# A one-core diffusion trunk on Trainium2: one weight load waits for a scatter, four matmul units change their place

## The reference

```python
for i in range(DEPTH):                                   # 4
    sh1, sc1, g1, sh2, sc2, g2 = split(silu(c) @ w_mod[i] + b_mod[i], 6)
    x = x + g1 * mixer_i(rmsnorm(x, norm_mix[i]) * (1 + sc1) + sh1)
    h = rmsnorm(x, norm_ffn[i]) * (1 + sc2) + sh2
    s = sigmoid(h @ w_router)                            # 384 x 16
    # best group of 4 experts, then the best two inside it; weights s, normalised
    # expert e: (silu(h @ w_gate[e]) * (h @ w_up[e])) @ w_down[e], 1024 -> 256 -> 1024
    x = x + g2 * sum_over_the_two_experts(weight * expert(h))
```

## Time and profile before

| | us |
|---|---|
| median of 3 runs | 1728.62 |
| lowest, highest | 1721.64, 1734.59 |
| the profiled execution | 1723.16 |
| its span, first to last instruction | 1721.3 |
| PE busy in the span | 1462.2 (85%) |
| mean granted clock of TensorE | 0.939 of full |

### The profile page before, as it was taken

One profiled execution on the slowest core, in us unless ns is written; L12 is line 12 of the kernel. 1 busy time (PEld: TensorE's weight loads), 2 busy tenths in 40 slices (PEclk: granted clock), 3 DMA queues, 4 the chain that ended last, 5 costly groups with the idle time before them and its releaser, 6 DMA issues.

```text
span 1721.3 us, 26508 instructions
## 1 busy us (share of the span) xinstructions
PE 1462.2 (85%) x10765; PEld 880.4 (51%) x10765; DVE 543.2 (32%) x1326; ACT 374.3 (22%) x985; POOL 197.5 (11%) x287
## 2 busy tenths in 40 slices
PE   2889897898997998598889988978989899979983
PEld 1766685232576676233374455843326666763321
DVE  0125624111526525011333343231105145251104
ACT  0104512111212622111120343211112035221101
POOL 0100021000213012010110000210101000120002
PEclk9899998899998998899999999978999999979987
DMA  9797045999959124799948323458998850358992
GB/s 343 268 321 262 2 150 195 362 420 422 323 218 318 22 98 157 314 399 420 393 172 274 70 74 127 143 234 306 422 418 297 268 191 2 123 203 302 421 413 100
DMA packets 125060, 428.70 MB, mean 249 GB/s; under 512 B 13124, under 2 KB 55063, under 8 KB 100359
## 3 DMA queue, kind: packets, MB, share of 16 engines
q1 hardware_dynamic: 96854, 350.32, 53.2%
q0 software_dynamic: 21136, 72.73, 12.6%
q10 hardware_dynamic: 6944, 3.91, 0.8%
HBM read 389.22 MB, written 40.26 MB: 250 GB/s over the span
## 4 chain that ended last, share of the span: by engine, by line
PE 66%; DMA 14%; DVE 8%; issue 5%; ACT 2%; POOL 2%; SPq 1%; DVEq 0%; ACTq 0%; POOLq 0%
PE bank L1666 58%; DMA work<-in_moe_w_gate 4%; DMA ring<-in_w_mod 4%; DMA h_slots<-xn,row_of 3%; PE bank L1829 3%; PE bank L1988 2%; DMA hT<-h_slots 1%; PE bank L1723 1%; ACT pp L1018 1%; POOL small L692 1%; POOL h_slots L797 1%; DVE xn L1165 1%; PE bank L1874 1%; DVE hT L1152 1%; SPq L602 1%
## 5 line engine op out<-in xcount | busy, mean ns | idle before, releaser
L1666 PE MATMUL bank<-ring,pp 128*32 128x512 f32 x2312 | 321.2, 604 | 11.3 <-issue 9.2
L1666 PE MATMUL bank<-ring,hT 128*128 128x256 f32 (+3 forms) x1142 | 271.3, 397 | 5.9 <-DVE hT L1152 3.3
L1666 PEld LDWEIGHTS bank<-ring,hT 128*128 128x128 f32 x1142 | 212.9, 195 | 61.2 <-issue 29.0
L1666 PE MATMUL bank<-work,pp 128*32 128x512 f32 x888 | 239.7, 624 | 2.7 <-DVE pp L1540 2.0
L1666 PE MATMUL bank<-ring,xn 128*128 128x256 f32 x768 | 168.2, 380 | 0.0
L1666 PEld LDWEIGHTS bank<-ring,pp 128*32 128x32 f32 x2312 | 88.5, 111 | 135.3 <-issue 134.3
L1666 PEld LDWEIGHTS bank<-ring,xn 128*128 128x128 f32 x768 | 145.0, 190 | 19.4
L1666 PE MATMUL bank<-V,pp 128*32 128x512 f32 x640 | 121.8, 623 | 25.5 <-issue 21.5
L1556 DVE TENSOR_TENSOR pp<-bank,pp 128x256 f32<-128x256 f32 x40 | 17.0, 425 | 339.2 <-ACT pp L1095 339.2
L1666 PE MATMUL bank<-ring,condT 128*32 128x256 f32 x1536 | 98.7, 403 | 17.2 <-DMA ring<-in_w_mod 17.2
L1018 ACT ACTIVATE pp<-bank,neg_max 128x384 f32<-128x384 f32 x192 | 95.6, 514 | 13.9 <-DVE neg_max L1447 10.1
(11 more groups left out here) (249 smaller groups left out, 1562.0 us busy)
## 6 DMA issues: line engine op xcount, KB each, us to landing
ring<-in_w_mod SPq DMA_DIRECT2D x96, 1024.0 KB, 8.9
ring<-in_moe_w_down SPq DMA_DIRECT2D x52, 1024.0 KB, 18.7
ring<-in_moe_w_gate SPq DMA_DIRECT2D x32, 1024.0 KB, 13.0
ring<-in_moe_w_up SPq DMA_DIRECT2D x32, 1024.0 KB, 15.3
hT<-h_slots POOLq DMA_DIRECT2D x36, 512.0 KB, 11.3
V<-in_moe_w_gate SPq DMA_DIRECT2D x16, 1024.0 KB, 13.7
V<-in_moe_w_up SPq DMA_DIRECT2D x16, 1024.0 KB, 17.0
work<-in_moe_w_gate SPq DMA_DIRECT2D x16, 1024.0 KB, 9.8
```

Source lines behind the costliest of these rows:

```text
L1666: return pe.matmul(out, lhsT, rhs, start=start, stop=stop)
```

## The change

SP waits for `h_out` of the layer (all six scatters landed) ahead of the gate unit of expert 3, in all four layers. On PE the first four "route" units run behind `hrow(2)` and ahead of the count of loads; the second four stay behind the ranks.

```diff
@@ sync
                 for key in moe_units(L):
+                    if key == ("moe_g", L, 3):
+                        sp.wait_ge(h_out, 96 * (L + 1))
                     if key[0] == "mod":
                         fill_mod(key)
                         continue
@@ tensor
                 hrow(2)
+                mods(mod_of["route"][:4])
                 pe.wait_ge(gates_ready, L + 1)
                 key = ("load", L)
...
                 done(mm(job_bank(key)[:, 32:48], ones[:, :], g48[:, 0:16], False, True))
-                mods(mod_of["route"])
+                mods(mod_of["route"][4:])
                 pe.wait_ge(mod_copied, min(6 * L + 8, 24))
```

## The result

| | us |
|---|---|
| after, median of 12 runs (lowest, highest) | 1715.1 (1706.2, 1720.4) |
| before beside it, median of 12 runs | 1728.7 |
| ratio, 95% interval | 0.9911 (0.9895 to 0.9927) |
| the profiled execution after | 1713.5, span 1711.7, clock 0.945 |

The change gains 0.89% (0.73 to 1.05), 15.4 us (12.6 to 18.2), against the 19.7 forecast. That ratio is one of means; the two medians lie 13.5 us apart. The direction and the mechanism held, the size came out a fifth smaller (by the medians a third), and the gain stays just short of 1%.

What follows compares the result with a forecast made beforehand. PE waits for block 1's gather behind a scatter slowed by SP's weights. 11.9 + 9.8 + 0.6 - 1.6 - 1.0 = 19.7 us takes the profiled 1723.2 to 1703.5, the median 1728.6 to 1709; range 1695 to 1727 (8 in 10).

Steps and rivals of the forecast that it cites:

- scatter in, layer 0: Last scatter of layer 0 lands at 301.7 instead of 302.3, gain 0.6 us; the hold has no grip there.
- layer 1: Last scatter of layer 1 lands at 694.6 instead of 706.5, with fewer weights beside it: gain 11.9 us.
- layer 2: Last scatter of layer 2 lands at 1150.8 instead of 1160.65, with fewer weights beside it: gain 9.8 us.
- gathers of layers 0 to 2: Block 1's gather stays at 8 us, again meeting a full SP queue (bounds 4.5 and 9): no gain.
- block 1 in layer 3: Three held loads run beside layer 3's gather, so block 1's gate-up starts later: loss 1.6 us (bounds 0 and 4).
- clock: After PE's idle time, block 1's gate-up in layers 1 and 2 runs slower, about 0.5 us each: loss 1.0.
- Rival (a): PE stays at half clock through the four early units, count 3.5 us late: gain 12.2, 1716.4 us; chance 0.17.
- Rival (c): Block 1's gather lands behind all 3.1 MB of released weights: 33 us lost against 21 gained, 1740 us; chance 0.08.
- Rival (b): Four weight units ahead still slow the scatter to its end: gain 2.9 us in all, 1726 us; chance 0.2.
- part 1: Four units moved ahead of the count on PE: count 1 us later (bounds 0 and 3.5), SP's slots back sooner.
- What starts expert 5 sooner shifts the rest by the same: DMA is saturated after expert 5's issue, so an earlier start carries through whole, if SP's queue is empty by then.
- The rule on queues: Round-robin between DMA queues: the hold helps only once SP's queue is dry; equal shares would make the gain 20.0 us.

Runs made afterwards that it cites:

- sets C and D: Kernel before the change, rerun unchanged on two chips: 1728.0 us (ratio 0.9998) and 1728.6 us (ratio 0.9996).
- set B: The changed kernel rerun unchanged on another chip: 1716.9 us, kernel before beside it 1716.9, ratio 0.9988.
- set C: Chip where the kernel before took 1728.5 us; against it, the hold with the four units left late, run again: 1727.2 us.
- sets A and B: Two chips, kernel before 1712.5 and 1716.9 us; against it, with units late: hold at gate of expert 3 1720.9, at down of expert 0 1715.0.

## Why the prediction was right, and where its sizes were off

The terms, from stretches between marks that all kernels pass (the router's copy to the landing of the scatter; to the issue of gate of expert 5), each a mean over three executions of before (the first, sets C and D) and two of after (the first, set B). Whether the stretch behind the turn is longer by the clock alone the marks don't tell:

| us gained | forecast | measured |
|---|---|---|
| scatter in, layer 0 | 0.6 | 1.0 |
| layer 1 | 11.9 | 8.3 |
| layer 2 | 9.8 | 9.3 |
| gathers of layers 0 to 2 | 0 | -2.1 |
| block 1 in layer 3 | -1.6 | -2.1 |
| clock; measured, block 1's turn to gate of expert 5 in layers 0 to 2 | -1.0 | -1.0 |
| the same stretch in layer 3 | 0 | 0.9 |
| sum, forecast; to gate of expert 5, measured | 19.7 | 14.3 |
| the whole | 19.7 | 15.4 (12.6 to 18.2) |

**The mechanism was right.** The earlier trace rows against the earlier trace rows said that the weights beside the scatter make it slow; fewer beside it made it fast in layers 1 and 2 of all six kernels that have early units and a hold. The two halves had to come together, as the prediction had it: early units alone 19.92 us in layer 1, the hold alone 16.6 (set C), both 10.96. Layer 0 gave nothing to speak of, and the hold had no grip there. Rival (a) fell: the clock did come back within the first four units (64 in 4.28 us, not twice 3.63), and the delay was 0.8 to 1.5 us in the first execution and 0.8 or less in the second, against 1 forecast. Rival (c) fell: gathers took 8.6 to 9.2 us in the first three layers, nowhere near 13. Rival (b), four units slow the scatter to its end, is wrong as it stood (it priced the gain at 2.9 us), but what it names is there: with two units ahead and not four the scatter of layer 1 takes half the time.

Of the signs that were named, these came: gate of expert 2 goes out ahead of the first scatter in layer 1, the wait ahead of the count is gone, layer 0's last scatter lands within 13 us (12.94), layer 3's gather lands after 1558 (1559.4 in the marks of before), block 2 doesn't wait for gate or up of expert 3, and the gain of layers 1 and 2 is still there when gate of expert 15 goes out (7.6 and 8.1 us). These didn't: the scatters of layers 1 and 2 take 10.96 and 10.37 us and not under 10, and the gathers over 8.

**Layer 1 was mis-sized by 3.6 us, for two reasons.** The first is the row itself: the earlier trace rows had the last scatter at 20.6 us, the two other executions 18.7 and 18.5. The mean from the copy to `h_out` is 40.2 us and not 41.8, so 1.6 us of the 11.9 weren't there to be gained. The second is the end of the scatter, as the profiled execution shows it. The forecast had the scatter in at 694.6; the marks of the profiled execution lie 2.4 us later, which makes it 697.0, and it came at 700.14. The sum let the last 3.9 scatters run at 1.27 us each with the engines full to the end, and landed them with the last byte. But 95% of the scatter's packets are through at 697.6. The rest, 0.4 us of work at 420 GB/s, trickle until 699.8, and the landing follows 0.3 us later: some 2.1 of the 3.1 us by this estimate. The rate is 0.8 us more: the engines moved 375 and 388 GB/s in 683 to 691 and not 420. That the scatter's bytes began over 4 us after the first issue, and not "about 2", was wrong as a reading of a lone scatter but cost little by itself, since the weights that had to go anyway had the engines for that time.

**Layer 2 looks better than it is.** The 9.3 against 9.8 leans on one slow execution of before (21.3 us, set C); the first pair of executions gives 8.7. And gate of expert 2, which waits for the first group's last unit, was put at about 1131, though by part 1's own terms that group ends at 1129.1 (count at 1128.1 and 1 us of delay). It went out 8.7 us after the copy, 1129.3 in the marks of before. So a start put too late and an end put too early partly cancelled, and that is luck.

**The gather was mis-sized by 0.6 to 0.9 us a layer.** "The gather then stays at 8 us" took the value of before (8.1, 8.2 and 8.0 as means); it became 8.7, 9.2 and 8.7, 2.1 in all. The upper bound, 9, was the better value.

**Layer 3**: block 1 is 2.1 us late, 1.6 forecast. **What is behind block 1** takes as long as before: the span less its start up to the first router's copy, and less the stretches from the copies to gate of expert 5, is 1239.5 us as a mean of before (1236.7, 1241.1, 1240.7) and 1243.0 of after (1238.6, 1247.4). The two after differ by 9 us from each other, so of a give-back of 0 to 4 us nothing is shown. "What starts expert 5 sooner shifts the rest by the same" holds at the change's size. Most of those 9 us, 6.7, lie in the last layer behind its gate of expert 5.

It doesn't hold further out. The stretches from gate of expert 5 to the next router's copy, layers 0 to 2 together (of the last four kernels one execution each):

| | copy to gate of 5, us | gate of 5 to the next copy, us | gate of 5 lands after its issue, us |
|---|---|---|---|
| before, three executions | 173.8 to 175.8 | 1083.4 to 1088.9 | 4.8 to 5.2 |
| the change, two | 161.5, 157.2 | 1086.6, 1088.7 | 4.7 to 5.0 |
| hold from down of 0 | 140.6 | 1089.9 | 7.2 to 9.0 |
| hold from gate of 3 until block 1 is in | 142.0 | 1091.7 | 8.8 to 8.9 |
| hold from down of 0 until block 1 is in | 128.8 | 1104.3 | 13.1 to 15.0 |
| hold from gate of 2 | 133.1 | 1102.1 | 13.7 to 15.7 |

Against the hold from gate of 3 until block 1 is in, the last two start expert 5 13 and 9 us earlier and lose 13 and 10 behind, more than the 6 us between executions of one kernel. (In the last layer, where none of these four holds, they lose 4 and 7 more, which isn't the hold's doing.) The last column suggests where it goes: the more was held back, the more stands in SP's queue ahead of expert 5's weights, and they land 13 to 16 us after their issue where 5 is usual. So held weights come late for the blocks after block 1. That this lateness is all of the loss is argued; no run separates it.

**The rule on queues.** The prediction weighed the Trainium skill's rule that each engine goes round-robin between the queues that have work, a packet at a time ("DMA: Bandwidth & Descriptors", "Queues, rings and completion order"), and read it as equal shares. The trace agrees with the rule and not with that reading: the queues take turns one packet for one (packets as the profile counts them), 143 and 143 before in 691 to 695, 128 and 116 after in 687 to 691, and the weights' packets are twice as large, so they have two thirds of the bytes. What the rule doesn't give is the time over 4 us ahead of that, with scatters issued, in which the weights have all.

## What to carry to other kernels

When a short transfer that the next step waits for shares the engines with bulk loads, count what is in the queue ahead at its issue, not only what is issued beside it: here a hold that began four units deep still left the scatter at twice the time it had with two. End the hold at the last short transfer of the chain, here the gather and not the scatter, and stop there; holding back more than that started the block earlier and lost as much again behind. And take the rows on which the largest term rests from more than one execution, and the baseline from more than one chip.

## What had not been expected

- In every layer where 1 MB or more of weights passes ahead of the first scatter's first byte (1.0 to 1.8 MB), that byte moves 4.3 to 5.1 us after the issue. On idle engines it is 1.7 to 1.8 us (all four layers of before). It is 1.7 and 1.9 too in layers 1 and 2 of both holds from down of 0, where the last 0.5 to 0.65 MB of weights were still passing. So a busy engine alone doesn't delay it; what does is open.
- Late modulation units stall on TensorE, 7.3 to 8.7 us for 64 matmuls instead of 3.63, with gaps that the profile calls issue, in all six groups of the two kernels with late units that were profiled on the chips of sets A and B, and in none of the twelve of the four other executions with late units (three of before, one of the hold alone). The transfers of instructions that the profile shows look alike in both kinds; the cause is open.
- The same program differs by chip: the kernel before takes 1728.5 to 1728.7 us in three sets and 1712.5 and 1716.9 in two, while the changed one takes 1715.1 and 1716.9.
